# A megabyte of expert weights more, loaded ahead of the first expert

## The chip, the cores and the metric

One core of one Trainium2 chip runs the whole layer. The metric is the device time of one execution in microseconds; the time before is the median of three runs.

## The reference

A hybrid encoder layer is applied to two requests of 256 tokens of width 2048, with shared weights. Cut to what matters:

```
h = x + W_out[ rms(NA(x_n)) ; rms(MLA(x_n)) ]          # attention part
hn = rmsnorm(h)
aff = softmax(hn @ w_router)                           # 16 experts
gates, idx = top_k(aff.T, 32)                          # each expert picks 32 tokens per request
hid = silu(hn[idx] @ w_gate[e]) * (hn[idx] @ w_up[e])  # 2048 -> 1024
y = h; y[idx] += (hid @ w_down[e]) * gates             # 1024 -> 2048
```

All numbers are fp32. The three weight matrices of one expert are 8 MB each, 384 MB for all 16 experts, and each is used once.

## The kernel before

The attention part comes first; each expert then reads its weights from HBM in 12 pieces of 2 MB: four of `w_gate`, four of `w_up`, four of `w_down`. The pieces are numbered on here over the experts, so expert 0 has the pieces 0 to 11 and expert 1 the pieces 12 to 23. All loads are issued by SyncE (SP) in an order written out by hand, on one queue; a wait of SP holds back all issues behind it.

The buffers are six ring buffers of 16 KB per partition (`ring`, in three pairs), and for the first two experts three more (`extra`), which stand where activations of the attention part and later `y` lie. So `AHEAD`, 9 pieces, can be loaded before an expert has begun. `place(e, i)` says which buffer a piece has: pieces 0 to 5 ring 0 to 5, pieces 6 to 8 extra 0 to 2, pieces 9 to 14 ring 0 to 5 again, 15 to 17 extra 0 to 2 again, and from 18 on the ring alone. From expert 2 on (piece 24) two pieces come in one load of 4 MB (`load_pair`).

TensorE counts up `piece_used` after each piece, and SP waits for the count that says that the buffer's last user is done. The loads of expert 0 are released by steps of the attention part's last chunk (L691 to L702). The first two buffers that come free in expert 0 are refilled in parts, while their pieces are still being used: `refill_first` (first issue at 774.75) loads piece 9 into ring 0 by quarters (L603) and `refill_second` piece 10 into ring 1 by halves (L615), by the count `first_used`, which goes up after each quarter of piece 0 and after half of piece 1. For expert 1:

```
for i in range(12):
    sp.wait_ge(piece_used, 12 + i + 1 - AHEAD)
    load_piece(e, i)
```

TensorE's order of work in an expert: eight pieces for gate and up (L1674), the gathering of the next expert's tokens (L1611), transposes, four pieces for down (L1657), and the scatter of a pair of experts (L1639) between the pieces of the next one. ScalarE writes `hid` after the eighth piece and VectorE multiplies it (L1299). The activations of one expert (`xe`, `xeT`, `hid`, `hidT`, `gT`, `gate1h`, 16 KB together) lie at `X0`, the last four of them in its second half. `gate1h` is set to zero once (L1342), before expert 0 on VectorE.

Of the kernel before, what the change touches and what calls it, by code (L numbers as in the profile page):

```python
# [33 lines left out]
P = 128  # L34
# [18 lines left out]
KB = 1024  # L53
# [13 lines left out]
def hybrid_layer(nc, t_in, outs):  # L67
# [8 lines left out]
    X0 = R0 + 64 * KB  # L76
# [56 lines left out]

    extra_at = [Q0, Q0 + 16 * KB, X0 + 16 * KB]
    extra = [at(f"extra{i}", [P, 4096], o) for i, o in enumerate(extra_at)]
    AHEAD = RING + len(extra)

    def packed(offset, limit):
# [57 lines left out]
    with ctx:  # L196
# [60 lines left out]
        piece_used = sem("piece_used")  # L257
        first_used = sem("first_used")
        refill_landed = sem("refill_landed")
        second_landed = sem("second_landed")  # L260
        pick_ready = sem("pick_ready")
        gate1h_ready = sem("gate1h_ready")
# [307 lines left out]
        def _(sp):  # L570
# [31 lines left out]
            def refill_first(i):  # L602

                dst, landed, _ = place(0, i)
                src = w_down[0].rearrange("(b p n c) f -> b n p (c f)", b=2, n=2, p=P)[i % 4 // 2, i % 2]
                for c in range(4):
                    if c < 3:
                        sp.wait_ge(first_used, c + 1)
                    else:
                        sp.wait_ge(piece_used, 1)  # L610
                    sp.dma_start(dst[:, 1024 * c:1024 * c + 1024], src[:, 1024 * c:1024 * c + 1024])\
                      .then_inc(refill_landed if c < 3 else landed, 16)

            def refill_second(i):

                dst, landed, _ = place(0, i)
                src = w_down[0].rearrange("(b p n c) f -> b n p (c f)", b=2, n=2, p=P)[i % 4 // 2, i % 2]
                for c in range(2):
                    if c == 0:
                        sp.wait_ge(first_used, 4)  # L620
                    else:
                        sp.wait_ge(piece_used, 2)
                    sp.dma_start(dst[:, 2048 * c:2048 * c + 2048], src[:, 2048 * c:2048 * c + 2048])\
                      .then_inc(second_landed if c == 0 else landed, 16)
# [63 lines left out]
            def load_expert(e):  # L688
                if isinstance(e, int) and e == 0:

                    wait_piece(sp, NP - 3)  # L691
                    load_piece(0, RING + 1)
                    load_piece(0, 0)
                    sp.wait_ge(lo_ready, NP)
                    load_piece(0, 2)
                    wait_piece(sp, NP - 2)
                    load_piece(0, 4 + NP % 2)
                    load_piece(0, RING + 2)
                    sp.wait_ge(acc_done, NT * NCH)
                    load_piece(0, 5 - NP % 2)  # L700
                    sp.wait_ge(folded, 2)
                    load_piece(0, 3)  # L702
                    refill_first(AHEAD)
                    refill_second(AHEAD + 1)
                    for i in range(AHEAD + 2, 12):
                        sp.wait_ge(piece_used, i - AHEAD + 1)
                        load_piece(0, i)
                elif isinstance(e, int) and e == 1:
                    for i in range(12):
                        sp.wait_ge(piece_used, 12 + i + 1 - AHEAD)  # L710
                        load_piece(e, i)
                else:
                    last = isinstance(e, int) and e == EXPERTS - 1
                    for i in range(0, 4 if last else 12, 2):
                        sp.wait_ge(piece_used, e * 12 + (i + 2 - RING))
                        load_pair(e, i)
                    for i in range(4, 12 if last else 4):
                        sp.wait_ge(piece_used, e * 12 + (i + 1 - RING))
                        load_piece(e, i)
# [288 lines left out]
        def _(dve):  # L1008
# [330 lines left out]
            take_xeT_half(0, 0)  # L1339
            take_gathered(0)  # L1340
            take_xeT_half(0, 1)
            then(dve.memset(gate1h[:, :, :, :, :, :], 0.0))  # L1342
            expert(0, 0, first=True)
            expert(0, 1)
            dve.wait_ge(y_set, NT)
            with dve.Fori(1, PAIRS - 1) as k:
# [7 lines left out]
        def _(pe):  # L1354
# [288 lines left out]
            def down(e, i, first):  # L1643

                a = i - 8
                w = landed(e, i)[:, :].rearrange("p (k n) -> p k n", n=D)
                if first and i == AHEAD:
                    pe.wait_ge(refill_landed, 48)
                if first and i == AHEAD + 1:
                    pe.wait_ge(second_landed, 16)  # L1650
                if a == 0 and not first:
                    pe.wait_ge(ye_first, 4 * e)
                    pe.wait_ge(ye_second, 4 * e)
                for k in range(2):
                    for h in range(2):
                        for n in range(2):
                            mm = pe.matmul(ps[64 * n:64 * n + 64, 2 + h, :],  # L1657
                                           hidT[:, 2 * (a % 2) + k, 64 * (a // 2):64 * (a // 2) + 64],
                                           w[:, k, 1024 * h + 512 * n:1024 * h + 512 * n + 512],
                                           start=a == 0 and k == 0, stop=a == 3 and k == 1)  # L1660
                mm.then_inc(piece_used, 1)

            def expert(k, i, first=False, more=True):

                e = 2 * k + i
                for m in range(8):
                    if m in (0, 2):

                        pe.wait_ge(xeT_ready, 2 * e + 1 + m // 2)
                    w = landed(e, m)[:, :].rearrange("p (c n) -> p c n", c=4)  # L1670
                    b, n = (m % 4) // 2, m % 2
                    for c in range(4):
                        for half in range(2):
                            mm = pe.matmul(ps[64 * half:64 * half + 64, m // 4, :], xeT[:, b, c, 64 * n:64 * n + 64],  # L1674
                                           w[:, c, 512 * half:512 * half + 512],
                                           start=m % 4 == 0 and c == 0, stop=m % 4 == 3 and c == 3)
                        if first and i == 0 and (m == 0 and c < 3 or m == 1 and c == 1):
                            mm.then_inc(first_used, 1)
                    mm.then_inc(piece_used, 1)
                    if first and i == 0 and m == 0:  # L1680
                        turn_xe_half(0, 1)
                    if i == 0 and not first:
                        if m == 0:

                            pe.wait_ge(ye_first, 8 * k)
                            pe.wait_ge(ye_second, 8 * k)
                            pe.wait_ge(gT_ready, k)
                            pe.wait_ge(hidT_ready, e)
                        if m >= 2:
                            pe.wait_ge(y_added, 8 * k + (m - 9))  # L1690
                        scatter(m)
                if i == 0 and not first:
                    pe.wait_ge(y_added, 8 * k)
                if more:
                    gather(e + 1)
                if i == 1:
                    pe.wait_ge(gate1h_ready, k + 1)
                    for g in range(NREQ):
                        for j in range(2):
                            mm = pe.transpose(ps[:, 6, P * (2 * g + j):P * (2 * g + j) + P],  # L1700
                                              gate1h[:, g, j, :, :, :].rearrange("p r i s -> p (r i s)"), ident)
                    mm.then_inc(gT_done, 1)
                pe.wait_ge(hid_ready, e + 1)
                for c in range(4):
                    mm = pe.transpose(ps[:, 7, P * c:P * c + P], hid[:, P * c:P * c + P], ident)
                mm.then_inc(hidT_done, 1)
                if more:
                    turn_xe(e + 1)
                pe.wait_ge(hidT_ready, e + 1)
                if more:  # L1710
                    for m in range(8, 12):
                        down(e, m, first)
                    return

                pe.wait_ge(ye_first, 4 * e)
                pe.wait_ge(ye_second, 4 * e)
                last_quarter(0, 0, 8)
                last_quarter(1, 0, 8)
                last_rounds(0)
                last_quarter(2, 0, 8)  # L1720
                last_rounds(1)
                last_quarter(3, 0, 4)
                last_rounds(2)
                last_quarter(3, 4, 8)
                last_rounds(3)
# [102 lines left out]
```

## Time and profile before

| | |
|---|---|
| median of three runs | 1693.71 us (1691.87 to 1694.28) |
| the profiled execution | 1692.41 us, its span 1690.6 us |
| TensorE busy | 1590.9 us, 94% of the span |
| DMA | 479.03 MB, mean 283 GB/s over the span |
| mean granted TensorE clock | 0.99 of full speed |

The profile shows one execution. Times in it are counted from the start of its span, in microseconds. The share of a busy engine is a mean over the whole span, so it is read beside the row of 40 equal slices of some 42.3 us, in which each digit is a tenth of busy time and a line for the bytes moved stands under them.

### The profile page before, as it was taken

The numbers are of one execution on the slowest core, as the hardware profiler recorded it, in microseconds if no ns is written. First come the engines' busy times: TensorE is split into PE (matmuls) and PEld (weight loads), VectorE is DVE, ScalarE is ACT, GpSimd is POOL, SyncE is SP. The second block draws the span as 40 slices with busy tenths as digits, with TensorE's granted clock in tenths as the row PEclk, the third lists the DMA queues.
The fourth block names the chain that finished last, engine by engine and source line by source line (L and its number), as shares of the span: only waits on it lengthen the run. The fifth ranks groups of instructions, "written<-read, shape, count | busy, mean of one in ns | idle before, by whom it ended". The sixth has DMA issues, their size and how long they took to land.

```text
span 1690.6 us, 18701 instructions
## 1 busy us (share of the span) xinstructions
PE 1590.9 (94%) x7902; PEld 923.7 (55%) x7902; DVE 537.7 (32%) x801; ACT 351.2 (21%) x562; POOL 24.0 (1%) x24
## 2 busy tenths in 40 slices
PE   8999999999999999999999899898998998998997
PEld 7888887888789788884333323223332332332233
DVE  3544323633886432322122022121221221220313
ACT  5422213623455522130000000000000000000000
POOL 1100000000000000000000000000000000000000
PEclk9999999999999999999999999999999999999999
DMA  8422331233220434268999999999999999999998
GB/s 301 130 86 88 108 100 55 50 107 93 84 74 1 175 126 148 75 273 330 429 418 430 429 431 434 433 430 431 430 433 433 431 431 430 433 433 431 433 424 323
DMA packets 81848, 479.03 MB, mean 283 GB/s; under 512 B 19424, under 2 KB 31840, under 8 KB 67968
## 3 DMA queue, kind: packets, MB, share of 16 engines
q1 hardware_dynamic: 80720, 475.45, 69.4%
q0 software_dynamic: 1072, 2.77, 0.8%
q8 instruction: 43, 0.70, 0.2%
q14 instruction: 13, 0.11, 0.0%
HBM read 473.07 MB, written 6.03 MB: 283 GB/s over the span
## 4 chain that ended last, share of the span: by engine, by line
PE 71%; DMA 23%; DVE 3%; ACT 1%; issue 1%; SPq 0%; DVEq 0%; ACTq 0%
PE ps L1674 18%; DMA ring_pair<-w_up 13%; PE ps L1403 11%; PE ps L1405 11%; PE ps L1404 11%; DMA ring_pair<-w_gate 9%; PE ps L1657 7%; PE ps L1639 3%; PE ps L1611 2%; PE ps L1491 2%; DMA ring_pair<-w_down 1%; PE ps L1540 1%; PE ps L1518 1%; PE ps L1528 1%; PE ps L1740 1%
## 5 line engine op out<-in xcount | busy, mean ns | idle before, releaser
L1674 PE MATMUL ps<-ring_pair,xeT 128*64 128x512 f32 x1968 | 454.1, 611 | 59.6 <-DMA ring_pair<-w_gate 31.9
L1674 PEld LDWEIGHTS ps<-ring_pair,xeT 128*64 128x64 f32 x1968 | 145.0, 140 | 361.0 <-issue 293.2
L1657 PE MATMUL ps<-ring_pair,hidT 128*64 128x512 f32 x944 | 206.0, 594 | 0.1
L1403 PE MATMUL ps<-w_hi,actT_hi 128*128 128x512 f32 x512 | 200.5, 392 | 2.0 <-DVE w_lo L1024 1.4
L1405 PE MATMUL ps<-w_hi,actT_lo 128*128 128x512 f32 x512 | 199.6, 390 | 0.0
L1404 PE MATMUL ps<-w_lo,actT_hi 128*128 128x512 f32 x512 | 199.4, 390 | 0.0
L1024 DVE TENSOR_TENSOR w_lo<-w_raw,w_hi 128x2048 fp32r<-128x2048 f32 (+1 forms) x56 | 126.2, 2254 | 210.1 <-ACT w_hi L793 210.1
L793 ACT ACTIVATE w_hi<-w_raw 128x2048 fp32r<-128x2048 f32 (+1 forms) x57 | 106.5, 1868 | 196.6 <-PE ps L1405 192.0
L1657 PEld LDWEIGHTS ps<-ring_pair,hidT 128*64 128x64 f32 x944 | 74.7, 137 | 122.0 <-issue 118.2
L1285 DVE TENSOR_TENSOR y<-y,ps 128x1024 f32<-128x1024 f32 x64 | 77.8, 1221 | 199.6 <-PE ps L1639 199.6
L968 ACT ACTIVATE hid<-ps 128x512 f32<-128x512 f32 x15 | 9.0, 597 | 512.3 <-PE ps L1674 512.3
L1403 PEld LDWEIGHTS ps<-w_hi,actT_hi 128*128 128x128 f32 x512 | 96.2, 188 | 22.2 <-issue 2.1
L1405 PEld LDWEIGHTS ps<-w_hi,actT_lo 128*128 128x128 f32 x512 | 96.2, 188 | 20.0
L1404 PEld LDWEIGHTS ps<-w_lo,actT_hi 128*128 128x128 f32 x512 | 96.2, 188 | 19.6
L1315 DVE COPY ye<-ps 32x512 f32<-32x512 f32 x60 | 41.5, 691 | 198.1 <-PE ps L1657 196.7
L1299 DVE TENSOR_TENSOR hid<-hid,ps 128x512 f32<-128x512 f32 x15 | 10.3, 685 | 231.2 <-ACT hid L968 231.2
L994 ACT ACTIVATE ye<-ps 32x512 f32<-32x512 f32 x60 | 35.3, 588 | 214.7 <-PE ps L1657 213.6
L1639 PE MATMUL ps<-ye,gT 64*128 64x512 f32 x256 | 71.2, 638 | 1.0 <-ACT ye L985 1.0
L1611 PE MATMUL ps<-h,pick1h 128*32 128x512 f32 x512 | 58.5, 596 | 10.7 <-DVE y L1285 9.8
L1403 PE MATMUL ps<-w_hi,mix_na 128*128 128x512 f32 x128 | 50.5, 395 | 1.9 <-DVE out_mla L1149 1.1
L1405 PE MATMUL ps<-w_hi,mix_na 128*128 128x512 f32 x128 | 50.0, 390 | 0.0
L1404 PE MATMUL ps<-w_lo,mix_na 128*128 128x512 f32 x128 | 49.9, 390 | 0.0
(232 smaller groups left out, 1502.2 us busy)
## 6 DMA issues: line engine op xcount, KB each, us to landing
ring_pair<-w_gate SPq DMA_DIRECT2D x28, 4096.0 KB, 19.0
ring_pair<-w_up SPq DMA_DIRECT2D x26, 4096.0 KB, 20.8
ring_pair<-w_down SPq DMA_DIRECT2D x26, 4096.0 KB, 20.7
w_raw<-w_in SPq DMA_DIRECT2D x31, 1024.0 KB, 5.3
w_raw<-w_out SPq DMA_DIRECT2D x16, 1024.0 KB, 5.1
ring_pair<-w_up SPq DMA_DIRECT2D x8, 2048.0 KB, 17.9
ring_pair<-w_down SPq DMA_DIRECT2D x8, 2048.0 KB, 20.3
ring_pair<-w_gate SPq DMA_DIRECT2D x7, 2048.0 KB, 12.6
```

The costliest lines, as they stand in the source:

```text
L793: act.activation(dst, src, ACT.Copy).then_inc(hi_ready, 1)
L994: act.activation(ye[32 * i:32 * i + 32, 512 * q:512 * q + 512], ps[64 * n:64 * n + 32, 2 + h, :], ACT.Copy).then_inc(ye_first, 1)
L1024: dve.tensor_tensor(dst, src, hi.bitcast(F32), ALU.subtract).then_inc(lo_ready, 1)
L1285: dve.tensor_tensor(v, v, ps[:, 4 + 2 * j:6 + 2 * j, :], ALU.add).then_inc(y_added, 1)
L1315: dve.tensor_copy(ye[64 + 32 * i:96 + 32 * i, 512 * q:512 * q + 512], ps[64 * n + 32:64 * n + 64, 2 + h, :]).then_inc(ye_second, 1)
L1403: pe.matmul(out, a_hi, hi[:, k, :], start=kk == 0, stop=False)
L1404: pe.matmul(out, a_hi, lo[:, k, :], start=False, stop=False)
L1405: mm = pe.matmul(out, a_lo, hi[:, k, :], start=False, stop=kk == ch["nk"] - 1)
L1611: mm = pe.matmul(ps[r:r + 32, 4 + b, :], pick1h[:, j, g, :], hid_x[:, 2 * g + j, 1024 * b:1024 * b + 1024] .rearrange("p (r n c) -> p n r ...
L1639: mm = pe.matmul(ps[:, 4 + 2 * j + g, :], gT[rows, g, j, :], ye[rows, 512 * q:512 * q + 512], start=True, stop=True)
L1657: mm = pe.matmul(ps[64 * n:64 * n + 64, 2 + h, :], hidT[:, 2 * (a % 2) + k, 64 * (a // 2):64 * (a // 2) + 64], w[:, k, 1024 * h + 512 * n: ...
L1674: mm = pe.matmul(ps[64 * half:64 * half + 64, m // 4, :], xeT[:, b, c, 64 * n:64 * n + 64], w[:, c, 512 * half:512 * half + 512], start=m ...
```

## The change

- Piece 7 (the eighth, the last of `w_up`) is loaded in two halves: the first into the first half of its buffer `extra[1]`, the second into `spare`, a new name for the 8 KB in which `hid`, `hidT`, `gT` and `gate1h` lie from expert 0's activation on. TensorE reads it from the two places. `spare` is loaded after the attention part's last matmul, ahead of piece 3.
- Piece 9 (the tenth, the second of `w_down`) is loaded in two halves: the first into the second half of `extra[1]`, ahead of expert 0, the second into the first half of ring 0, in two quarters, as the first two quarters of piece 0 have been used. The refill of ring 1 (piece 10) is issued at the same count of TensorE's work as before, under another number.
- Piece 16, which goes to `extra[1]`, has to wait until piece 9 is used (`piece_used` 10 in place of 8); the loads behind it on SP follow in order.
- The memset of `gate1h` moves from ahead of expert 0 to behind it.

```diff
+    spare = at("spare", [P, 2048], X0 + 8 * KB)
...
-                for c in range(4):
-                    if c < 3:
-                        sp.wait_ge(first_used, c + 1)
-                    else:
-                        sp.wait_ge(piece_used, 1)
-                    sp.dma_start(dst[:, 1024 * c:1024 * c + 1024], src[:, 1024 * c:1024 * c + 1024])\
-                      .then_inc(refill_landed if c < 3 else landed, 16)
+                for c in range(2):
+                    sp.wait_ge(first_used, c + 1)
+                    sp.dma_start(dst[:, 1024 * c:1024 * c + 1024], src[:, 2048 + 1024 * c:3072 + 1024 * c])\
+                      .then_inc(refill_landed if c < 1 else landed, 16)
+
+            def load_halves(i):
+
+                src = w_up[0].rearrange("(b p n c) f -> b n p (c f)", b=2, n=2, p=P)[i % 4 // 2, i % 2]
+                sp.dma_start(extra[1][:, 0:2048], src[:, 0:2048]).then_inc(extra_landed[1], 16)
+                src = w_down[0].rearrange("(b p n c) f -> b n p (c f)", b=2, n=2, p=P)[AHEAD % 4 // 2, AHEAD % 2]
+                sp.dma_start(extra[1][:, 2048:4096], src[:, 0:2048]).then_inc(ninth_landed, 16)
+
+            def load_spare(i):
+
+                src = w_up[0].rearrange("(b p n c) f -> b n p (c f)", b=2, n=2, p=P)[i % 4 // 2, i % 2]
+                sp.dma_start(spare[:, :], src[:, 2048:4096]).then_inc(spare_landed, 16)
...
-                        sp.wait_ge(first_used, 4)
+                        sp.wait_ge(first_used, 3)
...
-                    load_piece(0, RING + 1)
+                    load_halves(RING + 1)
...
                     load_piece(0, 5 - NP % 2)
+                    load_spare(RING + 1)
                     sp.wait_ge(folded, 2)
                     load_piece(0, 3)
...
-                        sp.wait_ge(piece_used, 12 + i + 1 - AHEAD)
+                        sp.wait_ge(piece_used, max(12 + i + 1 - AHEAD, AHEAD + 1 if 12 + i >= AHEAD + RING + 1 else 0))
...
-            then(dve.memset(gate1h[:, :, :, :, :, :], 0.0))
             expert(0, 0, first=True)
+            then(dve.memset(gate1h[:, :, :, :, :, :], 0.0))
...
+                w = [w[:, k] for k in range(2)]
                 if first and i == AHEAD:
-                    pe.wait_ge(refill_landed, 48)
+                    pe.wait_ge(refill_landed, 16)
+                    pe.wait_ge(ninth_landed, 16)
+                    w = [extra[1][:, 2048:4096], ring[0][:, 0:2048]]
...
+                    w = [w[:, c] for c in range(4)]
+                    if first and i == 0 and m == RING + 1:
+                        pe.wait_ge(spare_landed, 16)
+                        w[2:] = [spare[:, 1024 * c:1024 * c + 1024] for c in range(2)]
...
-                        if first and i == 0 and (m == 0 and c < 3 or m == 1 and c == 1):
+                        if first and i == 0 and (m == 0 and c < 2 or m == 1 and c == 1):
```

## Rows read from the trace of the kernel before

**Rows 1.** The page: engines' busy time, share and instructions; the 40 slices.

```profile
PE 1590.9 (94%) x7902; PEld 923.7 (55%) x7902; DVE 537.7 (32%) x801; ACT 351.2 (21%) x562; POOL 24.0 (1%) x24
...
GB/s 301 130 86 88 108 100 55 50 107 93 84 74 1 175 126 148 75 273 330 429 418 430 429 431 434 433 430 431 430 433 433 431 431 430 433 433 431 433 424 323
```

**Rows 2.** Chain that ended last, late part: start us, us, what.

```profile
1048.91 21.21 DMA ring_pair<-w_up
...
1643.42 21.94 DMA ring_pair<-w_down
```

**Rows 3.** Busy time by stretch; last columns PEclk, DMA share, GB/s.

```profile
1048.90:1165.20 116.30, 105.75 (x508) 36.55 (x508) 24.64 (x41) 8.28 (x14) 0.00 (x0) 0.99 1.00 431
...
768.00:776.00 8.00, 7.11 (x52) 2.37 (x52) 2.63 (x8) 1.88 (x2) 0.00 (x0) 1.00 0.06 16
776.00:780.00 4.00, 4.00 (x22) 1.34 (x19) 2.00 (x6) 0.00 (x0) 0.00 (x0) 1.00 0.98 298
860.00:864.00 4.00, 4.00 (x22) 1.33 (x20) 0.00 (x0) 0.00 (x0) 0.00 (x0) 1.00 0.74 246
802.05:814.15 12.10, 12.10 (x78) 4.64 (x80) 2.67 (x4) 1.79 (x3) 0.00 (x0) 1.00 1.01 431
```

**Rows 4.** TensorE's waits from 774 to 931; then its timeline from 933.

```profile
PE ps L1611 <- DVE y L1285: 1.4, 1, 1.4
...
934.15 1.41 PE L1674 MATMUL ps<-ring_pair,xeT 128*64 128x512 f32 x4 [2.03 <-DMA ring_pair<-w_gate]
```

**Rows 5.** Chain that ended last, experts 0 and 1: start us, us, what.

```profile
777.87 24.18 PE ps L1674 x112
...
820.98 27.46 PE ps L1674 x128
...
852.01 0.59 PE ps L1700 x4
...
853.91 13.88 PE ps L1657 x64
867.79 3.43 PE ps L1674 x16
```

**Rows 6.** SP's DMA issues: start of the first, us to the last one's end.

```profile
779.77 2.04 SPq L623 DMA_DIRECT2D ring_pair<-w_down  x2
...
798.66 0.33 SPq L595 DMA_DIRECT2D extra<-w_gate  x1
802.09 8.95 SPq L595 DMA_DIRECT2D extra<-w_up  x2
814.15 3.76 SPq L595 DMA_DIRECT2D ring_pair<-w_up  x2
...
861.10 0.34 SPq L600 DMA_DIRECT2D ring_pair<-w_gate  x1
```

**Rows 7.** Us to landing, issues at 729.01, 756.93, 774.75, 798.66, 802.09, 848.63, 861.10, 867.84.

```profile
extra<-w_up SPq DMA_DIRECT2D x1, 2048.0 KB, 8.5
ring_pair<-w_up SPq DMA_DIRECT2D x1, 2048.0 KB, 8.6
ring_pair<-w_down SPq DMA_DIRECT2D x1, 512.0 KB, 3.6
extra<-w_gate SPq DMA_DIRECT2D x1, 2048.0 KB, 17.1
extra<-w_up SPq DMA_DIRECT2D x1, 2048.0 KB, 18.5
ring_pair<-w_gate SPq DMA_DIRECT2D x1, 4096.0 KB, 16.0
ring_pair<-w_gate SPq DMA_DIRECT2D x1, 4096.0 KB, 14.7
ring_pair<-w_up SPq DMA_DIRECT2D x1, 4096.0 KB, 17.6
```

**Rows 8.** Groups by line, VectorE: busy us, mean ns, idle before.

```profile
L1342 DVE MEMSET gate1h<- 128x512 f32 x1 | 0.5, 485 | 0.1
```

More of the change, by code:

```diff
@@ L259, in hybrid_layer @@
         refill_landed = sem("refill_landed")
+        spare_landed = sem("spare_landed")
+        ninth_landed = sem("ninth_landed")
         second_landed = sem("second_landed")
@@ L1341, in _ @@
             take_xeT_half(0, 1)
+            expert(0, 0, first=True)
             then(dve.memset(gate1h[:, :, :, :, :, :], 0.0))
-            expert(0, 0, first=True)
             expert(0, 1)
@@ L1658, in down @@
                                            hidT[:, 2 * (a % 2) + k, 64 * (a // 2):64 * (a // 2) + 64],
-                                           w[:, k, 1024 * h + 512 * n:1024 * h + 512 * n + 512],
+                                           w[k][:, 1024 * h + 512 * n:1024 * h + 512 * n + 512],
                                            start=a == 0 and k == 0, stop=a == 3 and k == 1)
@@ L1674, in expert @@
                             mm = pe.matmul(ps[64 * half:64 * half + 64, m // 4, :], xeT[:, b, c, 64 * n:64 * n + 64],
-                                           w[:, c, 512 * half:512 * half + 512],
+                                           w[c][:, 512 * half:512 * half + 512],
                                            start=m % 4 == 0 and c == 0, stop=m % 4 == 3 and c == 3)
-                        if first and i == 0 and (m == 0 and c < 3 or m == 1 and c == 1):
+                        if first and i == 0 and (m == 0 and c < 2 or m == 1 and c == 1):
                             mm.then_inc(first_used, 1)
```

## The prediction, made before the changed kernel had run

> **What bounds the kernel now.** I read the page first. TensorE is busy for 94% of the span, but the slices show two different programs: over the first eighteen the DMA moves little, from the twentieth (803 us) on it moves some 430 GB/s without a break [rows 1]. Next the chain of work that ended last: late in the span its long pieces are weight loads of some 21 us, down to the last one at 1643.42 [rows 2]. The table of stretches says the same of one pair of experts: 116.3 us, DMA share 1.00, TensorE busy for only 105.75 us of it [rows 3]. The 24 pieces of that stretch are 24 x 2.097 MB = 50.3 MB, and 50.3 MB in 116.3 us is 433 GB/s. So the end is set by when the stream of weights arrives, and a shift of that stream in the steady part moves the end by the same amount.
>
> The question is then where the stream's position is fixed. The waits show no matmul that waits for a load between 774 and 931; the first one waits until 934.15 [rows 4]. Before that TensorE runs from piece to piece without a gap, 24.18 us for seven pieces, 3.45 us each [rows 5]. In that part the stream has two holes: 768 to 776, when all buffers are full and the expert's tokens are still being picked, and 860 to 864, with 246 GB/s [rows 3]. The second one is explained by the issues: the pair 26/27 is issued at 861.10, as soon as piece 21 is used at 860.9 (half of the 13.88 us that four pieces take from 853.91), while the pair 24/25 before it was already nearly through [rows 5, 6]. So from 774 to 861 TensorE leads, the DMA queue is full up and then runs dry, and only from 861 on is the stream continuous to the end. Whatever is gained before 861 is lost there unless TensorE also comes earlier.
>
> **The change part by part.** The bytes stay the same; 1 MB of them goes before 774.75. Piece 7 comes in two halves, the second into the 8 KB of `hid`, `hidT`, `gT` and `gate1h`; the first half of piece 9 sits beside piece 7's first half in `extra[1]`.
>
> *Loads ahead.* One more megabyte at 431 GB/s [rows 3] is 2.4 us, queued ahead of piece 3, the last load before the first hole. Piece 3 is through by about 768, where the hole begins; changed, by 770.4, and it lands some 3.7 us after its last byte (as below), at 774.1. TensorE needs it two pieces after 777.87, at 784.8 [rows 5]. The hole takes it: cost 0. Without that hole it would push piece 9 back by 2.4 us. The number of issues stays the same (one load became two, one is new, four quarters became two).
>
> *The refills.* Piece 9 loses two of its four quarters. But piece 10 is still issued at 779.77, when half of piece 1 is used [rows 6]: the same event under another count. The two quarters' 1.05 MB are through by about 779.5 at the 298 GB/s of 776 to 780 [rows 3], and the queue is empty until piece 10's bytes flow, some 1.4 us after the issue (as after 774.75, with next to nothing moved before 776 [rows 3]). Now the four quarters fill it to about 782, so the stream gains some 1 us here of the 2.4 us. TensorE, which waits for no load, gains nothing.
>
> *The new wait.* `extra[1]` now holds half of piece 9, so piece 16 waits for 10 used pieces instead of 8. Before, it is issued at 802.09; the tenth piece is used when piece 18 is issued, 814.15 [rows 6]. SP works in order, so piece 17 (issued some 8.6 us later than 16, near 810.7) is held behind it, and 16, 17 and 18 go out together at 814.15. The queue cannot cover this. Its last work, piece 15, is issued at 798.66 and lands at 798.66 + 17.1 = 815.8 [rows 6, 7], or 814.8 with the gain above; the mean engine is through some 3.5 us before a landing (860.9 against 864.6 for the pair 24/25, below). So the queue stands empty from about 811.3 to 815.6, where the trace of before is at 431 GB/s [rows 3].
>
> Price of it, by landings: piece 16 lands at 802.09 + 18.5 = 820.6 now. Into an empty queue a load of this size lands 8.5 or 8.6 us after its issue [rows 7], so at 814.15 + 8.55 = 822.7, which is 2.1 us later. From there seven more pieces and the pair 24/25 follow without a gap in both kernels: 864.6 (848.63 + 16.0) becomes 866.7 [rows 6, 7]. TensorE needs that pair at 867.79 [rows 5], so nothing stalls; piece 16 itself is needed at 820.98 + 4 x 3.43 = 834.7.
>
> *What the second hole gives back.* The pair 26/27 lands now at 861.10 + 14.7 = 875.8, 11.2 us after the pair before it; the next step, to 867.84 + 17.6 = 885.4, is 9.6 us [rows 6, 7], and 4.19 MB at 431 GB/s are 9.7 us. So 1.5 us of the 11.2 are the dry queue. In the changed kernel the queue isn't dry at 861.10, and the pair lands at 866.7 + 9.7 = 876.4: **+0.6 us**. By bytes instead of landings: the queue runs out now at about 860.9 and resumes at 862.6 (the window 860 to 864 lacks 4 x 0.185 = 0.74 MB, 1.7 us); changed, ten pieces (20.97 MB, 48.8 us at 430 GB/s) from 815.6 end at 864.4: **+1.8 us**. The difference is the slowest of the 16 engines, which sets a landing (864.6 against 860.9 in bytes). I take the middle, +1.2 us. Lower end: the pair 26/27 lands in an empty queue at 861.10 + 8.55 + 4.9 = 874.5, so -1.3 us; TensorE's own times are the same, so nothing earlier is possible. Upper end: the step that I call dry queue is something else and stays (+2.1), and an engine falls back by as much once more (+1.5): +3.6 us.
>
> A price for the restart is also in the Trainium skill (DMA: Bandwidth & Descriptors, Anatomy of one DMA): some 2.0 us fixed plus bytes over 436 GB/s, fitted on another issuing path. By it, an estimate, piece 16 would take 6.8 us and land at 821.0, only 0.4 us late, and the second hole would swallow all of it; the two rows with 8.5 and 8.6 us disagree with it by 1.7 us.
>
> *The rest.* The memset of `gate1h` is 0.49 us of VectorE [rows 8], moved from the start of expert 0 behind its end (820.98); the gates are transposed at 852.01 [rows 5], so 0; without that slack 0.5 us. Two more semaphore waits on TensorE are for loads that are through before the first hole and used after 798: 0. The halves of an operand change no matmul.
>
> **The sum.** The profiled execution took 1692.41 us for a span of 1690.6; with +1.2 it would be 1693.6. The median is 1693.71, 1.3 above that execution, so I predict 1693.71 + 1.2 = 1694.9. A difference of 0.2%, 3.4 us, is about what this kernel's measurement can tell from none.
>
> **The rivals.**
> *The megabyte counts in full.* Were the stream unbroken from 774.75 to the end, the end would come 2.4 us sooner: 1691.3. For it: DMA is the bound for most of the span. Against it: the issues at 779.77 and 861.10 hang on TensorE, which doesn't get faster. Even this is within 0.2%. Chance 0.07.
> *The second hole takes everything.* If piece 16 lands within 7.9 us of its issue, the pair 24/25 lands by 866.1 and the pair 26/27 at 875.8 as before: 1693.7. For it: the first quarter of 774.75, 0.52 MB, landed in 3.6 us [rows 7]; the other 1.57 MB of a whole piece would add 3.65 us at 430 GB/s, 7.25 in all. Against it: the two whole loads with 8.5 and 8.6 us. The rule of the Trainium skill above gives the same end. Chance 0.18.
> *Slower.* The hole after piece 15 is passed on undiminished and one engine falls back: the upper end, +3.6, 1697.3. It decides from the point where the pair 24/25 lands after 867.79, 1.1 us later than I expect: then TensorE waits and its releases come late as well. For it: only 1.1 us of slack; against: the dry queue that the 246 GB/s show. Chance 0.14.
> *My forecast*, +0.3 to +2.5 us: 0.61.
>
> **How the numbers follow.** Forecast, second rival and most of the first lie within 0.2%: 0.83. Faster 0.04, from the first rival with a favourable run; slower 0.13, from the third. The range runs from the lower bound to the upper one (1692.4 to 1697.3), widened by 0.9 below and 0.7 above since three runs of one kernel spread over 2.4 us: 1691.5 to 1698.0.
>
> **What would show it.** SP's issues of pieces 16 to 18 within a microsecond of each other at 814; a hole in the bytes from about 811 to 815.5, and a small one near 780; piece 16 landing near 822.7 and the pair 24/25 near 866.7; no hole left at 860 to 864; the pair 26/27 still issued at 861.1; TensorE's first wait for a load ending at 934.7 to 936. The prediction is wrong if piece 15 is still in flight at 815.5, if TensorE reaches piece 21 at another time than 860.9, or if the pair 24/25 lands after 867.8.

## The result, and the profile after

The changed kernel takes 1695.03 us (median of 22 runs, 1693.22 to 1696.59). The kernel before, run 22 times in all, has a median of 1692.10. The ratio is 1.0013, 95% interval 1.0007 to 1.0019: slower by some 2.2 us (1.2 to 3.2; the two medians lie 2.9 us apart), which is within the 0.2% that were named as no difference, and 1 us more than the 1.2 us forecast. That the forecast time, 1694.9 us, lies only 0.1 us from the median is luck: it started from 1693.71, the median of three runs, which is 1.6 us above that of 22, and added a cost that was too small. The profiled execution took 1695.05 us, its span 1693.2.

First the issues of SP in the profile after, then the landings of four of them (issued at 800.18, 815.67, 850.16 and 862.63), beside [rows 6, 7]:

```profile
781.30 2.04 SPq L635 DMA_DIRECT2D ring_pair<-w_down  x2
...
800.18 0.33 SPq L598 DMA_DIRECT2D extra<-w_gate  x1
815.67 0.80 SPq L598 DMA_DIRECT2D extra<-w_up  x2
816.52 2.91 SPq L598 DMA_DIRECT2D ring_pair<-w_up  x2
...
850.16 0.35 SPq L603 DMA_DIRECT2D ring_pair<-w_gate  x1
...
862.63 0.34 SPq L603 DMA_DIRECT2D ring_pair<-w_gate  x1
```

```profile
extra<-w_gate SPq DMA_DIRECT2D x1, 2048.0 KB, 16.7
extra<-w_up SPq DMA_DIRECT2D x1, 2048.0 KB, 7.4
ring_pair<-w_gate SPq DMA_DIRECT2D x1, 4096.0 KB, 18.4
ring_pair<-w_gate SPq DMA_DIRECT2D x1, 4096.0 KB, 15.6
```

TensorE's use of the pieces 20 to 23 and of piece 24, from the chain that ended last, and its waits for loads from 774 to 931:

```profile
855.43 13.88 PE ps L1673 x64
869.32 3.43 PE ps L1694 x16
```

```profile
PE ps L1694 <- DMA ring_pair<-w_up: 0.6, 2, 0.4
```

Pieces 16, 17 and 18 leave together, one right behind the other, 15.5 us after piece 15. The stretches of the same profile (columns as in [rows 3]) show what that did to the stream:

```profile
776.00:780.00 4.00, 4.00 (x22) 1.48 (x20) 0.57 (x1) 0.00 (x0) 0.00 (x0) 1.00 0.69 215
780.00:784.00 4.00, 4.00 (x20) 1.29 (x18) 0.95 (x5) 0.00 (x0) 0.00 (x0) 1.00 0.57 178
808.00:812.00 4.00, 4.00 (x22) 1.58 (x22) 1.29 (x2) 0.37 (x1) 0.00 (x0) 1.00 1.03 438
812.00:816.00 4.00, 4.00 (x22) 1.40 (x20) 0.00 (x0) 0.00 (x0) 0.00 (x0) 1.00 0.30 127
816.00:820.00 4.00, 4.00 (x22) 1.33 (x20) 0.00 (x0) 0.00 (x0) 0.00 (x0) 1.00 0.85 303
860.00:864.00 4.00, 4.00 (x21) 1.29 (x19) 0.00 (x0) 0.00 (x0) 0.00 (x0) 1.00 1.08 467
864.00:868.00 4.00, 4.00 (x22) 1.42 (x20) 0.00 (x0) 0.00 (x0) 0.00 (x0) 1.00 0.94 401
```

A dip near 780 (178 GB/s from 780 to 784, where the megabyte that is already there is missing), a hole from 812 to about 816.5 (127 and 303 GB/s in place of 431), and no second hole, where 860 to 864 had 246 GB/s before [rows 3]: 467 and 401 GB/s from 860 to 868. (The second hole belongs to the issue of the pair 26/27, so where expert 0 begins later, the hole would lie as much later; the window from 864 on is shown for that.) That is the picture that the prediction drew.

But every time is about 1.5 us later than drawn, from the begin of expert 0 on. The chain that ended last shows why, here for the kernel before and then for the one after:

```profile
762.72 5.41 PE ps L1569 x42
...
773.69 3.58 PE ps L1674 x16
```

```profile
763.37 6.38 PE ps L1582 x42
...
775.22 3.58 PE ps L1694 x16
```

The 42 entries are the warm-up matmuls that TensorE does while the experts' tokens are picked. They began 0.65 us later and took 1 us longer in the execution after. So expert 0 begins at 775.22 in place of 773.69. The longer warm-up goes with a lower granted clock in this stretch (column PEclk; before, then after):

```profile
758.00:762.00 4.00, 2.71 (x20) 2.18 (x17) 2.36 (x10) 2.13 (x5) 0.00 (x0) 0.84 0.88 352
762.00:766.00 4.00, 3.89 (x27) 3.83 (x28) 3.29 (x12) 0.00 (x0) 0.00 (x0) 0.74 1.03 438
```

```profile
758.00:762.00 4.00, 3.22 (x19) 2.98 (x19) 1.79 (x7) 2.44 (x5) 0.00 (x0) 0.75 0.97 348
762.00:766.00 4.00, 3.98 (x20) 3.62 (x20) 3.23 (x13) 0.00 (x0) 0.00 (x0) 0.50 0.98 410
```

0.50 is the lower of the two levels, 1.2 GHz, granted after TensorE stood idle for 0.8 of the 4 us from 758 to 762; in the execution before, where it stood idle for 1.3 of them, the mean of 0.74 lies between the two levels, so part of these 4 us ran at 2.4 GHz. Two profiled executions can't say whether that belongs to the change. To compare, the times below are also counted from the begin of expert 0: from there to the end of the execution 1692.41 - 773.69 = 918.72 us before and 1695.05 - 775.22 = 919.83 us after, 1.1 us more.

### The profile page after: what moved, and what is told of

Read it like the earlier page. It is cut to its first block, busy times and chain, and to the rows that moved or that the text cites. A ratio compares the mean times of both kernels' runs of the same rounds, so it can differ in the third digit from the quotient of the medians.

```text
span 1693.2 us, 18702 instructions
## 1 busy us (share of the span) xinstructions
PE 1594.7 (94%) x7902; PEld 925.9 (55%) x7902; DVE 537.2 (32%) x801; ACT 351.4 (21%) x562; POOL 24.0 (1%) x24
## 4 chain that ended last, share of the span: by engine, by line
PE 72%; DMA 23%; DVE 3%; ACT 1%; issue 1%; SPq 0%; DVEq 0%; ACTq 0%
PE ps L1694 17%; DMA ring_pair<-w_up 13%; PE ps L1416 11%; PE ps L1418 11%; PE ps L1417 11%; DMA ring_pair<-w_gate 8%; PE ps L1673 7%; PE ps L1652 3%; PE ps L1624 2%; PE ps L1504 2%; DMA ring_pair<-w_down 1%; PE ps L1553 1%; PE ps L1531 1%; PE ps L1541 1%; PE ps L1760 1%
## 6 DMA issues: line engine op xcount, KB each, us to landing
ring_pair<-w_gate SPq DMA_DIRECT2D x7, 2048.0 KB, 12.6
```

## The experiments

The theory: the stream's only loss is the wait of piece 16 for 10 used pieces; the second hole gives part of it back; the megabyte ahead is worth nothing, since TensorE leads up to 861. The rivals: the change itself delays TensorE's begin of expert 0 (traffic, memset); the megabyte is worth 2.4 us and something else eats it; or the loss has no part given back. Ten runs were made, three of them of one of the two kernels without an edit. All times are medians beside the runs of before on the same chip.

**The kernel before again, as a measure.** No edit.

> The kernel before, unchanged, as a measure of what two equal kernels differ by, and as a second look at the time at which TensorE begins expert 0 (773.69 in the profile of before, 775.22 in that of after, where the warm-up matmuls ahead of it ran longer at half clock). Ratio 1.000 within 0.0006. If the begin of expert 0 moves by a microsecond between executions of one kernel, the 1.5 us of the profile of after need not come from the change; if it lies at 773.7 again, the rival that the change itself delays TensorE gains.

1692.19 us, ratio 0.9997 (0.9988 to 1.0006). Expert 0 begins at 773.49, so this profile supports the rival; time from there 918.98 us.

**The spare half alone.** The changed kernel without the first half of piece 9 ahead and without the longer wait:

```diff
-    for c in range(2):
-        sp.wait_ge(first_used, c + 1)
-        sp.dma_start(dst[:, 1024 * c:1024 * c + 1024], src[:, 2048 + 1024 * c:3072 + 1024 * c])\
+    for c in range(4):
+        if c < 3:
+            sp.wait_ge(first_used, c + 1)
+        else:
+            sp.wait_ge(piece_used, 1)
+        sp.dma_start(dst[:, 1024 * c:1024 * c + 1024], src[:, 1024 * c:1024 * c + 1024])\
...
-    sp.dma_start(extra[1][:, 2048:4096], src[:, 0:2048]).then_inc(ninth_landed, 16)
...
-    sp.wait_ge(piece_used, max(12 + i + 1 - AHEAD, AHEAD + 1 if 12 + i >= AHEAD + RING + 1 else 0))
+    sp.wait_ge(piece_used, 12 + i + 1 - AHEAD)
...
```

> The spare half of piece 7 and the later memset stay, but piece 9 is refilled by quarters as before and piece 16 waits for 8 again. My theory (the new wait is the whole cost of the stream, the megabyte ahead is worth nothing): no difference from before, 0 +- 1 us, second hole at 860 to 864 as before, begin of expert 0 anywhere between 773.5 and 775.5. Rival (the traffic of the spare half into 757 to 771, or the moved memset, delays TensorE): +1.5 us without any wait.

1692.08 us, ratio 0.9996 (0.9988 to 1.0005); 254 GB/s from 860 to 864, so the second hole is there; begin at 773.61:

```profile
860.00:864.00 4.00, 4.00 (x20) 1.29 (x18) 0.00 (x0) 0.00 (x0) 0.00 (x0) 1.00 0.74 254
```

The load into the small buffers and the moved memset have no cost that stands out of this interval.

**The wait alone.** The kernel before with one line of the change:

```diff
-    sp.wait_ge(piece_used, 12 + i + 1 - AHEAD)
+    sp.wait_ge(piece_used, max(12 + i + 1 - AHEAD, AHEAD + 1 if 12 + i >= AHEAD + RING + 1 else 0))
```

> Before, with nothing changed but the wait of piece 16 for 10 used pieces in place of 8. My theory: the cost of after, +0.6 to +1.8 us, with the same hole of some 3 to 4 us near 812 to 815.6 and no second hole. Rival (the cost of after comes from the rest of the change: TensorE's later begin, the moved memset, the halves): 0. Other rival (nothing is given back by the second hole): +3 to +4 us.

1695.24 us, ratio 1.0014 (1.0005 to 1.0023): as slow as the whole change, with nothing loaded ahead. Its stretches show the hole and the filled second one:

```profile
812.00:816.00 4.00, 4.00 (x22) 1.31 (x20) 0.00 (x0) 0.00 (x0) 0.00 (x0) 1.00 0.63 270
816.00:820.00 4.00, 4.00 (x22) 1.42 (x20) 0.00 (x0) 0.00 (x0) 0.00 (x0) 1.00 0.70 246
...
860.00:864.00 4.00, 4.00 (x20) 1.29 (x18) 0.00 (x0) 0.00 (x0) 0.00 (x0) 1.00 0.96 410
```

The two windows of the hole lack (430 - 270) x 4 + (430 - 246) x 4 = 1.38 MB, 3.2 us at 430 GB/s. Begin at 775.74, from there 919.72 us. The ratio stands for +2.4 us (0.8 to 3.9), above the +1.8 us of the expectation, and the interval holds both that and the +3 to +4 us of the other rival. So this run settles that the wait is the cost, but not whether part of it is given back; the landings below do.

**The megabyte ahead without the long wait.** The changed kernel with the buffers of pieces 16 and 17 swapped, so that piece 16 waits for 9 used pieces:

```diff
-    return extra[n - RING], extra_landed[n - RING], 16 * (lap + 1)
+    x = (0, 2, 1)[n - RING] if lap else n - RING
+    return extra[x], extra_landed[x], 16 * (lap + 1)
...
-    sp.wait_ge(piece_used, max(12 + i + 1 - AHEAD, AHEAD + 1 if 12 + i >= AHEAD + RING + 1 else 0))
+    sp.wait_ge(piece_used, 12 + i + 1 - AHEAD + (12 + i in (AHEAD + RING + 1, AHEAD + RING + 2)))
```

> After, but piece 16 goes to the third extra buffer (waits for 9 used pieces) and piece 17 to the second (waits for 10), so that the megabyte is still loaded ahead and the queue gets piece 16 at about 810.7 instead of 814.15. My theory: the hole near 812 shrinks from 4.3 us to at most 1 us, the second hole at 860 to 864 is back, the time is that of before (0 +- 0.8 us), 2 us below after. Rival (the megabyte counts in full once the wait is out of the way): 2.4 us below before.

1692.25 us, ratio 0.9995 (0.9986 to 1.0004). The hole at 812 to 816 shrinks to 303 GB/s for 4 us (1.2 us lost, a little over the 1 us expected), and the second one is back, 1.7 us later than in the profile of before, as expert 0 begins 1.7 us later:

```profile
812.00:816.00 4.00, 4.00 (x20) 1.29 (x18) 0.00 (x0) 0.00 (x0) 0.00 (x0) 1.00 0.86 303
816.00:820.00 4.00, 4.00 (x22) 1.40 (x20) 0.00 (x0) 0.00 (x0) 0.00 (x0) 1.00 1.01 430
...
860.00:864.00 4.00, 4.00 (x22) 1.29 (x18) 0.00 (x0) 0.00 (x0) 0.00 (x0) 1.00 0.93 360
864.00:868.00 4.00, 4.00 (x21) 1.30 (x19) 0.00 (x0) 0.00 (x0) 0.00 (x0) 1.00 0.83 328
```

The last two windows lack 0.69 MB, 1.6 us at 430 GB/s, against 1.7 us in the one window of before. A megabyte ahead of the first expert and no cost, but no 2.4 us either (they would be a ratio of 0.9986, the very edge of the interval). Begin at 775.35: a late begin occurs without the wait for 10 as well.

**Twice as long a wait.** The kernel before, piece 16 waiting for 12 used pieces:

```diff
-    sp.wait_ge(piece_used, 12 + i + 1 - AHEAD)
+    sp.wait_ge(piece_used, max(12 + i + 1 - AHEAD, AHEAD + 3 if 12 + i >= AHEAD + RING + 1 else 0))
```

> Before, with piece 16 waiting for 12 used pieces (end of expert 0, 47.3 us after its begin) in place of 8. The hole in front of piece 16 grows from about 3 to about 10 us. My theory (the second hole at 860 to 864 gives back at most its own 1.7 us, and that has been spent with the wait for 10): the extra 6.9 us are passed on in full, first stall of TensorE earlier than 934, +8 to +9.5 us against before. Rival (the queue has more slack further on, so the cost stays near the +2.5 us of the wait for 10): +2 to +5 us.

1701.83 us, median of five runs, ratio 1.0051 (1.0038 to 1.0065), some 8.6 us (6.4 to 11.0). Its stretches, and TensorE's first wait for a load, from its waits between 774 and 943:

```profile
812.00:816.00 4.00, 4.00 (x22) 1.36 (x20) 0.00 (x0) 0.00 (x0) 0.00 (x0) 1.00 0.53 225
816.00:820.00 4.00, 4.00 (x22) 1.37 (x20) 0.00 (x0) 0.00 (x0) 0.00 (x0) 1.00 0.00 0
820.00:824.00 4.00, 4.00 (x20) 1.29 (x18) 1.38 (x2) 1.36 (x3) 0.00 (x0) 1.00 0.26 53
```

```profile
PE ps L1674 <- DMA ring_pair<-w_gate: 6.1, 1, 6.1
```

From the begin of expert 0 (775.26) to the end it is 926.86 us. Against the 919.72 of the shorter wait that is 7.1 us more for an issue that is 822.58 - 775.26 - (816.19 - 775.74) = 6.9 us later: passed on in full. TensorE's wait of 6.1 us is at 875.55, at the pair 24/25, the point at which the third rival was to decide.

**TensorE later.** The kernel before with 14 more warm-up matmuls:

```diff
+            stay_warm(14)
             gather_part(0, 0, 0)
```

> Before, with 14 more warm-up matmuls of 128 columns on TensorE ahead of expert 0's gathering, some 3 us of which 0.9 us fall into a wait that is there anyway, so that expert 0 begins 2.1 us later at the same loads. My theory (TensorE leads from 774 to 861 and every issue hangs on it): +2 us at the end, the pair 26/27 issued 87.4 us after the begin of expert 0 as always. Rival (the stream of loads leads there and has the slack to take it): 0 to +0.5 us.

1694.94 us, ratio 1.0014 (1.0005 to 1.0023). Chain and issue of the pair 26/27:

```profile
777.97 3.58 PE ps L1674 x16
```

```profile
865.38 0.34 SPq L600 DMA_DIRECT2D ring_pair<-w_gate  x1
```

865.38 - 777.97 = 87.41 us, as before (861.10 - 773.69). With no byte and no wait of the loads changed, the end comes later, by the ratio 2.4 us (0.8 to 3.9) where 2.1 us were planned. The profiled execution begins 4.3 us later than that of before, since the planned delay and a late begin come together in it, and ends 3.1 us later.

**The begin again.** The changed kernel again, and the kernel before a third time:

> After, unchanged, for a second look at the begin of expert 0 and at the time from there to the end. My theory: from the begin of expert 0 to the end of the execution 919.8 us as in the two looks with the wait (918.7, 919.0, 917.5 and 917.0 in the four without), whatever the begin is. Rival (the later begin of expert 0, 775.2 and 775.7, belongs to the wait): begin at 775 or later again. Median 1695 +- 0.7 us.

> Before once more, one look only, for the begin of expert 0 (773.7 and 773.5 in the first two looks) and the time from there to the end (918.7, 919.0). My theory says nothing of the begin, which follows the granted clock of TensorE in the idle stretch before it; the rival that the wait comes with a late begin expects 773.6 +- 0.2.

1694.76 us, ratio 1.0009 (1.0000 to 1.0018), and in the one execution of the kernel before 1692.38 us. The begins, from the chain of the changed kernel and from that of the kernel before:

```profile
775.10 3.58 PE ps L1694 x16
```

```profile
775.45 3.58 PE ps L1674 x16
```

The changed kernel begins late again, as the rival expected, but so does the kernel before, where the rival expected 773.6. The kernels with a longer wait alone, which up to there equal the kernel before, begin at 775.74 and 775.26. So the begin moves by 2 us with nothing changed ahead of it, and the 1.5 us between the two first profiles need not come from the change. The rival that the change delays TensorE falls by the times: the swapped version has all of the change that stands ahead of expert 0, and takes no longer than before. From the begin to the end it is 919.81 us in the changed kernel and 916.93 in the one before.

**The second hole closed.** Piece 26 issued by itself when piece 20 is used, 27 when 21 is used; once on the swapped version, once on the changed kernel. For that the loads of expert 2 are taken out of the loop of SP:

```diff
+    if isinstance(e, int) and e == 2 and i == 2:
...
+        sp.wait_ge(piece_used, 21)
+        sp.dma_start(ring[2][:, :], src[1, 0]).then_inc(half_landed, 16)
+        sp.wait_ge(piece_used, 22)
+        sp.dma_start(ring[3][:, :], src[1, 1]).then_inc(pair_landed[1], 16)
+        continue
...
+    load_expert(2)
-    with sp.Fori(2, EXPERTS - 1) as e:
+    with sp.Fori(3, EXPERTS - 1) as e:
...
+    if i == 0 and not first and m == 2:
+        pe.wait_ge(half_landed, 16)
```

> The swap of the two extra buffers (no long wait of piece 16), and piece 26 issued by itself when piece 20 is used (some 3.5 us earlier), piece 27 when piece 21 is used, so that the queue isn't dry at 861. My theory (the second hole is worth its 1.3 to 1.7 us, and until then TensorE leads): no hole at 860 to 864, and from the begin of expert 0 to the end 0.8 to 1.7 us less than the 916.9 to 919.0 of the six looks without the wait, so 1691.3 +- 0.9 us. Rival (the megabyte ahead counts once both holes are closed): -3 us or more against before.

> After, with piece 26 issued by itself in the same way. My theory (with the wait for 10 the queue isn't dry at 861, so there is nothing left to close): no gain, 919.8 +- 0.2 us from the begin of expert 0 to the end, 1695 us. Rival (the second hole is there in both kernels and hasn't been spent): 1.5 us less than after.

On the swapped version 1692.35 us, ratio 1.0000 (0.9991 to 1.0009): no gain that can be measured, and just above the 1691.3 +- 0.9 us expected. The rival, 3 us or more, lies outside the interval (1.5 us either way). The profile, whose expert 0 begins at 777.27, has no second hole:

```profile
860.00:864.00 4.00, 4.00 (x22) 1.39 (x20) 0.00 (x0) 0.00 (x0) 0.00 (x0) 1.00 0.99 426
864.00:868.00 4.00, 4.00 (x22) 1.34 (x20) 0.00 (x0) 0.00 (x0) 0.00 (x0) 1.00 0.90 385
```

From the begin it takes 916.33 us, the lowest of all, but that begin is the second latest. On the changed kernel 1694.74 us, ratio 1.0010 (1.0001 to 1.0019), 919.60 us from the begin: nothing is gained, as expected where the queue isn't dry.

All profiled executions beside each other: how long the pair 26/27 took to land after its issue, and the time of the execution less the begin of expert 0.

| piece 16 waits for | kernels | begin of expert 0 | landing of the pair 26/27 after its issue | from the begin to the end |
|---|---|---|---|---|
| 8, 9 | before (3), spare alone, swap, TensorE later | 773.49 to 777.97 | 14.7, 15.0, 14.3, 13.2, 12.6, 13.5; mean 13.9 | 918.72, 918.98, 916.93, 917.45, 917.01, 917.55; mean 917.8 |
| 9, second hole closed | 1 | 777.27 | 12.5 (piece 27) | 916.33 |
| 10 | after (2), wait alone, after with the hole closed | 775.07 to 775.74 | 15.6, 15.7, 15.7, 15.7 (piece 27) | 919.83, 919.81, 919.72, 919.60; mean 919.7 |
| 12 | 1 | 775.26 | 22.6 | 926.86 |

The shortest and the longest of the six without the long wait (swap, and the second profile of before), and the second one of after:

```profile
ring_pair<-w_gate SPq DMA_DIRECT2D x1, 4096.0 KB, 12.6
ring_pair<-w_gate SPq DMA_DIRECT2D x1, 4096.0 KB, 15.0
ring_pair<-w_gate SPq DMA_DIRECT2D x1, 4096.0 KB, 15.7
```

This landing carries the difference to the end. The pair is issued 87.41 us after the begin in every profile in which it goes out as one load (piece 27 by itself at 87.27), and from its landing to the end it is 816.6 to 817.0 us in eleven of the twelve, 815.2 in the third profile of before.

## Why the prediction was right, and which term was off

*What sets the time.* Right: 87.4 us lie between the begin and the issue of the pair 26/27 in all the profiles, and the kernel with more warm-up matmuls ended later by about its delay. That each microsecond of a later begin reaches the end is not shown: the three profiles of before begin at 773.69, 773.49 and 775.45 and take 1692.41, 1692.47 and 1692.38 us, as what happens from that issue on differs by as much.

*The signs of being wrong.* By the clock of the profile all three of them came: piece 15 landed at 800.18 + 16.7 = 816.9, piece 21 was used at 862.4 (half of the 13.88 us from 855.43), the pair 24/25 landed at 868.6. Counted from the begin of expert 0, for which the prediction took the time of the profile of before, none did: 41.7 us against 41.8 (815.5 less 773.69), 87.2 us as before, and 93.3 us against 94.1. One sign that the forecast named did fail: TensorE's first waits for a load end at 888.01 and 897.72, 0.6 us together, not at 934.7 to 936; they are for pieces of `w_up`, stand in all four profiles with the wait for 10 and in none without it.

*The loads ahead are worth nothing.* Right: piece 10 is issued at 781.30 - 775.22 = 6.08 us after the begin, as before (779.77 - 773.69), the stream dips in front of it, and the swapped version, which keeps the megabyte and loses the long wait, is as fast as before. The first rival falls. Its remainder, a gain under the interval of 0.0009, is not excluded.

*The new wait is the cost.* Right, and shown by itself: that one line makes the kernel before as slow as the changed one.

*The restart.* Mis-sized. Piece 16 lands 7.4 us after its issue, not 8.55, so only 0.95 us late against the begin (47.85 against 820.6 - 773.69 = 46.9). That meets the second rival's condition (within 7.9 us), but its conclusion doesn't follow. The estimate by the Trainium skill (DMA: Bandwidth & Descriptors, Anatomy of one DMA), 6.8 us, was nearer than the two rows of before, but no landing of a whole piece here was as short. Piece 18, issued at 816.52 behind the others, lands 17.8 us later, at 834.3: from piece 16 to 18 it is 11.2 us where two pieces of data are 9.8. The pair 24/25 then lands at 850.16 + 18.4 = 868.6, 93.3 us after the begin, where it was 90.9: 2.4 us late, close to the 2.1 of the sum. TensorE needs it at 869.3, so the slack was 0.8 us, and TensorE did not wait there, which the third rival needs.

*What the second hole gives back.* The pair 26/27 lands at 862.63 + 15.6 = 878.2, 103.0 us after the begin; before it was 102.1. So +0.9 us, between the +0.6 by landings and the +1.8 by bytes, and 1.1 us at the end of these two executions. The forecast of +1.2 us is right for the executions whose profiles were compared. Over all profiles the cost is 919.7 - 917.8 = 2.0 us, and by the runs 2.2. The term that was too small is this one: the landings of one profiled execution of the kernel before were taken as its usual ones, but that execution (918.72) is among the longer ones of those without the wait, which spread over 2 us. There the pair 26/27 landed 14.7 us after its issue, and the mean of the six is 13.9, so 0.8 us were missing: 1.2 + 0.8 = 2.0. Against that mean the pair lands 1.8 us later with the wait (15.7), as the sum by bytes alone had it. The pair 24/25, issued 74.9 us after the begin in all of them, lands 15.6 us after its issue on the mean of the six and 18.4 us in the three with the wait, 2.9 us later; so the second hole gave back some 1.1 us.

*The wait's limit.* As the longer wait shows, the queue gives back only once: with the second hole spent, the further 6.9 us went to the end in full.

Open: the executions without the wait spread over 2 us, for the most part because the load that goes into the drained queue at the second hole lands 12.6 to 15.0 us after its issue, where with the wait for 10, and no second hole, it is 15.6 or 15.7. Why it varies is not shown; the views show no single one of the 16 engines. Nor is it settled whether closing the second hole is worth the expected 0.8 to 1.7 us; one profile and an interval of 0.0009 can't say.

## What to carry to other kernels

A buffer shared by two pieces is free only when the later of the two has been used. Before a preload is put there, look at the next tenant of the buffer and at what stands behind its wait on the same queue: here 2.4 us of loading ahead bought nothing, and the wait cost 2 us.

Before loading further ahead, see whether the consumer waits for loads. Here TensorE, in the kernel before, waited for none until 934, and the bytes moved earlier turned up as idle time of the queue, at the next issues that TensorE released (781.30 in the changed kernel, 862.76 in the swapped version).

For changes of 0.1%, one profiled execution of each kernel isn't enough, and a time that agrees to 0.1 us can be two errors that cancel: count from an event behind which both do the same work, and take more than one profile.

## What was not expected

The begin of expert 0 lies between 773.49 and 777.27 us in eleven profiles of kernels whose TensorE work up to there is the same. The granted clock falls after a short idle stretch in some of these executions (a mean of 0.74 of full speed from 762 to 766 in the first profile of before, 0.50 in that of after) and not in others: in the second profile of before and in that of the spare half alone, which begin at 773.49 and 773.61, it stays at 1.00 from 758 to 770, with 1.6 and 1.5 us of the 4 us from 758 to 762 idle.

A 2 MB load into the drained queue near 815 us landed 7.4 to 7.7 us after its issue in the six profiles that have one, where two such loads before expert 0 took 8.5 and 8.6 us [rows 7]; the price of a restart of the stream isn't one number.
